# Scaling attention weights with a diagonal matrix in the transposing product

## What is computed

```
def block_attention(q, k, v):            # 16 heads of 64, 4 key/value heads
    s = einsum('bkgqd,bskd->bkgqs', q_blk, k) * scale
    p = softmax(s, axis=-1)
    return einsum('bkgqs,bskd->bkgqd', p, v)

def cross_attention(h, mem_n, wq, wkv, wo):   # 4 heads of 256, 256 memory rows
    s = einsum('bshd,bmhd->bhsm', q, k) * (1.0 / sqrt(XA_HEAD_DIM))
    p = softmax(s, axis=-1)
    o = einsum('bhsm,bmhd->bshd', p, v)
    return o.reshape(B, S, D_MODEL) @ wo

def encoder_layer(x, mem, ...):
    x = x + (g_attn * attn_branch + g_sg * sg_branch) @ w_out
    x = x + cross_attention(rmsnorm(x), rmsnorm(mem), ...)
    x = x + peer_ffn(rmsnorm(x), ...)    # top 16 of 16384 experts per head
    return x
```

## Time and profile before

| | us |
|---|---|
| median of 3 runs | 2955.6 |
| lowest and highest | 2954.28, 2955.69 |
| profiled execution, its own time | 2953.1 |
| its span in the trace | 2951.3 |

### The profile page before, as it was taken

The page is one execution under the profiler, slowest core; times in us unless marked ns, Lnnn a source line. Parts: engine busy times, 40 slices in busy tenths (PEclk is TensorE's granted clock), DMA queues, the critical chain, the costliest instruction groups (busy, mean ns, idle before and its releaser), DMA issues. The chain is left out here.

```text
span 2951.3 us, 39042 instructions
## 1 busy us (share of the span) xinstructions
PE 2464.2 (83%) x12865; PEld 2127.5 (72%) x12865; DVE 2301.6 (78%) x4186; ACT 1153.2 (39%) x1928; POOL 1335.0 (45%) x1058
## 2 busy tenths in 40 slices
PE   6978877199988888979850665899999999999997
PEld 5856767188866667767640554799999998999996
DVE  6465437867569686656898776799999999999998
ACT  4453433133237323332111998333333333333333
POOL 0000001604531333423466320677777787777774
PEclk9989889599989999999965777899999999999998
DMA  4625433137862676736211764999999999999997
GB/s 150 219 104 178 154 128 109 47 115 263 316 212 79 213 279 239 284 114 229 103 45 44 265 229 175 360 400 401 401 399 399 400 401 401 400 398 400 400 400 278
DMA packets 231175, 747.60 MB, mean 253 GB/s; under 512 B 20864, under 2 KB 70192, under 8 KB 214400
## 3 DMA queue, kind: packets, MB, share of 16 engines
q0 software_dynamic: 112256, 408.71, 36.9%
q1 hardware_dynamic: 118784, 337.22, 31.4%
HBM read 708.09 MB, written 37.75 MB: 253 GB/s over the span
## 5 line engine op out<-in xcount | busy, mean ns | idle before, releaser
L1629 POOL DMA_INDIRECT rows<-in_up,now x384 | 588.5, 1533 | 182.6 <-issue 96.5
L186 DVE TENSOR_TENSOR w_lo<-w_raw,w_hi 128x2048 fp32r<-128x2048 f32 x116 | 269.2, 2322 | 341.8 <-ACT w_hi L180 341.2
L145 POOL DMA_INDIRECT row_ring<-in_down,IDX x208 | 281.9, 1355 | 547.9 <-DVE dots L136 509.7
L201 PE MATMUL lin<-w_hi,T_hi 128*128 128x512 f32 x976 | 395.3, 405 | 59.1 <-PEq L606 9.5
L1737 DVE SCALAR_TENSOR_TENSOR Y<-rows,dots,Y 128x1024 f32<-128x1024 f32 x320 | 404.0, 1276 | 14.3 <-DMA rows<-in_up,now 13.3
L202 PE MATMUL lin<-w_lo,T_hi 128*128 128x512 f32 x976 | 391.2, 401 | 0.0
L203 PE MATMUL lin<-w_hi,T_lo 128*128 128x512 f32 x976 | 390.6, 400 | 0.0
L180 ACT ACTIVATE w_hi<-w_raw 128x2048 fp32r<-128x2048 f32 x116 | 221.6, 1912 | 384.4 <-PE lin L203 363.6
L201 PE MATMUL tr<-T_hi,d_hi 128*128 128x384 f32 x1024 | 344.7, 337 | 14.6 <-DVE d_lo L1710 14.6
L203 PE MATMUL tr<-T_hi,d_lo 128*128 128x384 f32 x1024 | 344.8, 337 | 0.0
L202 PE MATMUL tr<-T_lo,d_hi 128*128 128x384 f32 x1024 | 344.1, 336 | 0.0
(11 more groups left out here) (218 smaller groups left out, 4977.4 us busy)
## 6 DMA issues: line engine op xcount, KB each, us to landing
w_raw<-in_wall SPq DMA_DIRECT2D x116, 1024.0 KB, 5.4
shared<-in_downT SPq DMA_DIRECT2D x128, 512.0 KB, 16.3
shared<-in_up SPq DMA_DIRECT2D x128, 512.0 KB, 16.3
dense_gates<-shared SPq DMA_DIRECT2D x12, 2048.0 KB, 7.5
wd<-dense_gates SPq DMA_DIRECT2D x32, 768.0 KB, 28.4
rows<-in_up,now POOLq DMA_INDIRECT x384, 9.8
row_ring<-in_down,IDX POOLq DMA_INDIRECT x208, 6.0
Y<-in_x SPq DMA_DIRECT2D x6, 512.0 KB, 4.8
```

Source lines behind the costliest of these rows:

```text
L145: pool.indirect_dma_start(self.ring[:, r % self.K, :], None, self.table, bass.IndirectOffsetOnAxis(ap=self.IDX[:, r:r + 1], axis=0)).then_ ...
L186: dve.tensor_tensor(self.lo[:, h % 2], self.raw[:, h % 2], self.hi[:, h % 2].bitcast(F32), ALU.subtract).then_inc(self.lo_done, 1)
L201: pe.matmul(out, lhs[0], rhs[0], start=start, stop=False, skip_group_check=True)
L1629: pool.indirect_dma_start(rows[:, k, :], None, table, bass.IndirectOffsetOnAxis(ap=now[:, j % 2, k:k + 1], axis=0)).then_inc(rows_in[k], 16)
```

## The change

The probabilities are no longer multiplied with the reciprocal of their sum before they are turned. DVE multiplies the 128x128 identity with the reciprocals, row by row, into a new tile `weight`, and PE multiplies with this diagonal matrix where it transposed before: with out = lhsT.T @ rhs, the probabilities as lhsT and diag(1/sum) as rhs, the result is the transposed and normalised block. The instruction is a matmul with start and stop in place of a transpose. The order on each engine, the semaphores and their counts are the same.

```diff
@@ attention (cross-attention)
+        weight = m.sb(f"{tag}_weight", [P, 3, P])
@@ turn(u)
                     for kb in range(width_of(units[u]) // P):
-                        last = pe.transpose(lin[:, 3 + u % 3, kb * P:(kb + 1) * P],
-                                            probs[:, u % 3, kb * P:(kb + 1) * P], ident[:])
+                        last = pe.matmul(lin[:, 3 + u % 3, kb * P:(kb + 1) * P], probs[:, u % 3, kb * P:(kb + 1) * P],
+                                         weight[:, u % 3, :], start=True, stop=True, skip_group_check=True)
@@ norm(u)
-                    w = width_of(units[u])
-                    dve.tensor_scalar(probs[:, i, 0:w], probs[:, i, 0:w], rr[:, i:i + 1], None,
-                                      ALU.mult).then_inc(normed, 1)
+                    dve.tensor_scalar(weight[:, i, :], ident[:], rr[:, i:i + 1], None, ALU.mult).then_inc(normed, 1)
@@ self_attention
+        weight = m.sb("att_weight", [P, 3, 2, P])
@@ turn(p)
                         for kb in range(q.nt):
-                            last = pe.transpose(lin[:, 4 + e, kb * P:(kb + 1) * P],
-                                                probs[:, p % 3, e, kb * P:(kb + 1) * P], ident[:])
+                            last = pe.matmul(lin[:, 4 + e, kb * P:(kb + 1) * P], probs[:, p % 3, e, kb * P:(kb + 1) * P],
+                                             weight[:, p % 3, e, :], start=True, stop=True, skip_group_check=True)
@@ norm(p)
-                        dve.tensor_scalar(probs[:, i, e, 0:w], probs[:, i, e, 0:w], rr[:, i, e:e + 1], None,
+                        dve.tensor_scalar(weight[:, i, e, :], ident[:], rr[:, i, e:e + 1], None,
                                           ALU.mult).then_inc(normed, 1)
```

## The result

| | median us | lowest, highest | profiled execution, its span |
|---|---|---|---|
| before, 6 runs | 2955.64 | 2951.87, 2960.22 | 2953.1, 2951.3 |
| changed, 6 runs | 2982.65 | 2978.12, 2985.04 | 2983.5, 2981.7 |

The ratio is 1.0087, 95% interval 1.0075 to 1.0098: the change makes the kernel slower by 26 us (22 to 29). Forecast were 2978 and slower, range 2965 to 2994.

A forecast was written before the change was run, and what follows sets the result against it. DVE was taken to bound self-attention and PE cross-attention, with PE the bound after the change. 15.5 + 3.0 + 4.2 = 22.7 us on 2953.1 gave 2975.8, against the median 2978; range 2965 to 2994.

The forecast's parts named there:

- The price of a product: PE's turning: a full fp32 product has two records and costs 0.225 us, a transposition one record and 0.11.
- A: Rival, PE's turning: the product costs hardly more than the transposition; 14.9 us saved, 2941; chance 0.04.
- D: Rival, PE's turning: the product costs four times the transposition, 0.44 us; +96 us, 3049; chance 0.03.
- C: Rival, attention stages: waits stay on top of the longer turning, nothing is absorbed; +40 us, 2996; chance 0.08.
- the ends: Start and end of the self-attention stages, where no room exists: 1.4 us more in the sample, 1.2 in the prompt.
- Sample's self-attention: PE sets the step at 3.98 us instead of 3.54, 32 steps, 14.1 us, plus 1.4 at the ends: +15.5.
- The gap of 0.20 to the values: Sample's self-attention on PE: 0.20 us between the last turning start and the first of values, kept unchanged.
- Prompt's self-attention: PE needs 2.30 us a step against 2.19, 1.8 us over 16 steps, plus 1.2 for the ends: +3.0.
- Cross-attention: PE is the bound; two products a unit, 24 units, 5.4 us at most, less 1.2 for waits: +4.2.
- DVE's gain: Shorter normalisation saves DVE 0.40 us a sample step, 0.13 a prompt step; decides nothing if PE is the bound.

The follow-up runs named there:

- product_twice: The changed kernel with each product of the turning issued a second time to the same place; ratio 1.0354 to the kernel before.
- diagonal_alone: Kernel before, with DVE scaling the 128-column identity but PE transposing with the plain identity, so the division is left out; ratio 0.9978.
- product_alone: Kernel before, with only the transposition replaced by a full fp32 product with the identity, DVE normalising as before; ratio 1.0084, 2982.8 us.
- diag_fp32r: The changed kernel with probabilities and diagonal held as fp32r, a reduced-precision form, in self- and cross-attention; ratio 1.0038 to the kernel before.

## Why the prediction was right, point by point

**The price of a product** (0.225 against 0.11, two records for one): right. Records of L754 and L624 doubled, and product_twice charges 0.225. The factor is 2; the Trainium skill ("TensorE: Matmul & The Clock Gate", Terms) has the transpose mode four times faster for fp32, and here the measurement decides: twice. Rivals A and D, which were about this price, did not come. D's own time was summed too low: cross-attention has two products a unit, so its term is 16 and not 8, and D would have been near 3060. C's term for the prompt is 0.38 a step by the prediction's own numbers, not 0.44, and the low end of the forecast's own range comes to 2972 and not 2967 (11.4 + 1.1 + 3.9 us at 0.107 a record and without the ends); neither changes which rival the result belongs to.

**Sample's self-attention**, +15.5: measured 18.8. PE's step was put at 3.98 and is 4.07. The gap of 0.20 to the values held. What the sum lacks is the first distance inside the group: the second record starts 0.21 after the first, and the prediction took fifteen equal distances of 0.1125. With it, 0.21 + 14 x 0.112 + 0.20 = 1.98. Two more things were off: every fourth step waits for the copy and is 0.28 longer, which the sum has at nothing, and the mean step before is 3.51 over the 27 steps from 876.38 to 971.20, not 3.54. These 27 steps grew by 16.7 us (94.8 to 111.6), the two ends by 0.9 and 1.2.

**Prompt's self-attention**, +3.0: measured 5.35. PE's own step came as worked out, 2.32 for 2.30. What failed is "2.30 against 2.19 now", that PE's sum is the step: every second one has 0.27 more, with the turning waiting for the copy. That is rival C in small. The eleven steps that took 23.96 before take 26.88 (171.54 to 198.42), 2.9 us more where the forecast has 0.11 each, 1.2; the ends took 2.4, of which 1.7 at the start, where 1.2 was taken for both. diagonal_alone shows that this stage was held by the loop of waits and not by DVE's sum, which the prediction read from a DVE without gaps.

**Cross-attention**, +4.2: measured 2.7. In the sample it is 2.2: the twelve units from 1287.86 to 1311.13 (1317.05 to 1342.33 in the changed kernel) grew by 2.0, since two waits for the copy shrank from 0.42 to 0.20 us, as the prediction had it, and the two ends grew by 0.2 together. In the prompt it is only 0.5 for 8 units, less than the forecast allowed for: from the stage's start to the scores of the fifth unit it took 8.03 us before and after (395.02 to 403.05, 400.64 to 408.67), and from the eighth's to the last values 5.00 (409.19 to 414.19, 415.28 to 420.28); the whole 0.5 lies in the three units between, of which one took 2.18 before.

**DVE's gain is worth nothing**: right, by product_alone. It would have been worth some 6 us and not 15 had the product cost no more than the transposition, by diagonal_alone; so rival A's 2941 was too low as well.

The sum was 22.7 and the stages say 26.8: the misses of 3.3, 2.4 and -1.5 partly cancel, and that part of the agreement is luck. The mechanism, PE's second record per block, is what product_alone, product_twice and diag_fp32r show.

## What to carry to other kernels

To fold a scaling into a transposition of fp32 blocks on PE trades a shorter instruction of DVE for a second record per block on PE; compare the prices as distances between starts, and count the room per step on PE (here 0.43 us for 8 blocks, 0.054 each, against 0.11) before making the trade. An engine without gaps is not thereby the bound: lighten it alone, in an experiment, and see whether the step follows. And work that fills a pipeline in every second step also sets how its end is reached: taking the row products out shortened the stage's last wait by 6 us, almost as much as its steps.

## What the runs showed of the hardware

An fp32r product of 128x128 by 128 columns is one record. In a group of eight the starts lie 0.119 us apart on average ((1.11 - 0.275) / 7 in diag_fp32r), no less than those of fp32 transpositions (0.117 by the same working).

Where a group of turning records follows half-array scores, the distance to its second record was 0.21 us and the one out to the half-array values 0.20, against 0.112 inside the group. In cross-attention, where all are full-array, four records of the turning and the step to the values took 0.44 us together (1322.33 to 1322.77), with no such addition.

With fp32r products in place of the transpositions, the prompt's self-attention ran at 1.2 GHz (granted clock 0.50) for its whole length in two kernels, though PE was busy 93 to 97% of the windows shown in one and 96 to 100% in the other, while with full fp32 products or with transpositions it reached 2.4 GHz. The Trainium skill ("TensorE: Matmul & The Clock Gate", Part 4) says that the full clock does not engage for the transpose mode; here the prompt's self-attention with transpositions had 1.00 from 185 to 202 us, but plain products stand between its transpositions, so this does not test that sentence.

The normalisation on DVE takes 0.487, 0.353 and 0.287 us for 512, 256 and 128 fp32 columns, linear with a start-up of 0.22.
